# Hybrid decoder layer on one core: the recurrence's outputs computed in two token halves inside the mixing block

## The reference

```
y     = wkv7_scan(r, decay, k, v, kk, a)          # 8 heads x 64, state S: S = S*w + sa kk*a + v k, y = S r
mu    = mean(y over the 64 of a head); var = mean((y-mu)^2)
yn    = (y - mu) * rsqrt(var + GN_EPS) * lnx_g + lnx_b
bonus = sum(r * k * r_k over a head) * v
y_rwkv = (yn + bonus) * g                          # g = sigmoid(xg) @ gate_g2
mix   = concat(y_rwkv, y_mla) @ w_out              # y_mla: causal attention, 8 heads x 64
x     = LayerNorm(ALPHA * x + mix)
x     = LayerNorm(ALPHA * x + relu(x @ w_ffn1)^2 @ w_ffn2)
```

## Time and profile before

| what | value |
|---|---|
| time, median of 3 runs | 1475.28 us (1472.87 to 1477.7) |
| the profiled execution's own time | 1473.56 us |
| its span | 1471.8 us |
| PE busy | 1393.8 us, 95% |
| DVE, ACT, POOL busy | 917.3, 451.8, 463.6 us |
| mean granted TensorE clock | 0.972 |

### The profile page before, as it was taken

One profiled execution on the slowest core, in us unless ns is written; L12 is line 12 of the kernel. 1 busy time (PEld: TensorE's weight loads), 2 busy tenths in 40 slices (PEclk: granted clock), 3 DMA queues, 4 the chain that ended last, 5 costly groups with the idle time before them and its releaser, 6 DMA issues. The chain is left out here.

```text
span 1471.8 us, 24860 instructions
## 1 busy us (share of the span) xinstructions
PE 1393.8 (95%) x10608; PEld 1145.3 (78%) x10608; DVE 917.3 (62%) x1017; ACT 451.8 (31%) x619; POOL 463.6 (32%) x285
## 2 busy tenths in 40 slices
PE   6999999888999979999789988999999999999997
PEld 5877878766777669997478876888888888888886
DVE  3547745254465424434747778777777685778887
ACT  2133533122433433232300352222121353433330
POOL 0000212120133110000105658666667344455030
PEclk8999999988999989999989999999999999999999
DMA  5111234486447952221061205444443897655653
GB/s 206 43 50 38 110 133 143 139 179 212 114 115 243 232 136 46 46 47 60 0 228 43 101 29 179 157 158 157 150 158 122 291 329 267 193 187 198 201 189 126
DMA packets 144830, 211.80 MB, mean 144 GB/s; under 512 B 79472, under 2 KB 82160, under 8 KB 144080
## 3 DMA queue, kind: packets, MB, share of 16 engines
q1 hardware_dynamic: 144528, 209.69, 44.9%
q10 hardware_dynamic: 192, 0.52, 0.2%
HBM read 136.18 MB, written 64.29 MB: 136 GB/s over the span
## 5 line engine op out<-in xcount | busy, mean ns | idle before, releaser
L2342 PE MATMUL banks<-stage_b_hi,stage_a_hi 128*128 128x512 f32 x448 | 174.3, 389 | 0.0
L2342 PE MATMUL banks<-stage_b_lo,stage_a_hi 128*128 128x512 f32 x448 | 174.3, 389 | 0.0
L2342 PE MATMUL banks<-stage_b_hi,stage_a_lo 128*128 128x512 f32 x448 | 174.3, 389 | 0.0
L2584 DVE TENSOR_TENSOR stage_a_lo<-stage_a_raw,stage_a_hi 128x1024 fp32r<-128x1024 f32 x56 | 98.7, 1762 | 38.7 <-ACT stage_a_hi L2438 38.7
L358 PE MATMUL banks<-xT_hi,win_hi 128*128 128x512 f32 x320 | 103.5, 405 | 4.7 <-DVE xT_lo L705 4.7
L358 PE MATMUL banks<-xT_lo,win_hi 128*128 128x512 f32 x320 | 100.4, 395 | 0.0
L358 PE MATMUL banks<-xT_hi,win_lo 128*128 128x512 f32 x320 | 100.0, 394 | 0.0
L2342 PEld LDWEIGHTS banks<-stage_b_hi,stage_a_lo 128*128 128x128 f32 x448 | 84.1, 188 | 17.6
L2342 PEld LDWEIGHTS banks<-stage_b_hi,stage_a_hi 128*128 128x128 f32 x448 | 84.1, 188 | 17.5
L2342 PEld LDWEIGHTS banks<-stage_b_lo,stage_a_hi 128*128 128x128 f32 x448 | 84.1, 188 | 17.3
L2438 ACT ACTIVATE stage_a_hi<-stage_a_raw 128x1024 fp32r<-128x1024 f32 x56 | 59.4, 1060 | 117.8 <-DMA stage_b_raw<-in_w_ffn 97.7
(11 more groups left out here) (404 smaller groups left out, 3683.5 us busy)
## 6 DMA issues: line engine op xcount, KB each, us to landing
stage_b_raw<-in_w_ffn SPq DMA_DIRECT2D x50, 512.0 KB, 4.7
hid_s<-tile_s SPq DMA_DIRECT2D x64, 256.0 KB, 4.3
stage_a_raw<-hid_s SPq DMA_DIRECT2D x32, 512.0 KB, 3.7
w_landed<-in_w_ffn SPq DMA_DIRECT2D x30, 512.0 KB, 5.1
hid_h<-tile_h SPq DMA_DIRECT2D x48, 256.0 KB, 2.0
stage_a_raw<-hid_h SPq DMA_DIRECT2D x24, 512.0 KB, 3.8
win_raw<-in_w_in SPq DMA_DIRECT2D x20, 512.0 KB, 3.7
x_tok<-in_x SPq DMA_DIRECT2D x8, 512.0 KB, 8.0
```

Of the source, the lines that this page charges most:

```text
L2342: last = nc.tensor.matmul(ps[:, bank, :], s[a][:, j, tok], s[b][:, j, :], start=p == 0 and j == 0 and n == 0, stop=p == NP - 1 and j == 1 ...
L2584: V.tensor_tensor(s["a_lo"][:], s["a_raw"][:], s["a_hi"][:].bitcast(F32), ALU.subtract).then_inc(lo2, 1)
```

## The change

1. `rwkv_chunks`: `v` is turned to tokens by `centre`, the identity less 1/64 within a head, so the values are centred on entry; TensorE waits once for VectorE to make it. The outputs go into an own tile `y_all`. SP loads three row tiles of `w_out` at the end of its list.
2. The block `rwkv_outputs` is gone. Its work stands in `mix_ffn`, in two halves `h` of 512 tokens, without the means and their subtraction. The dot product is written over `hT`'s key rows and the bonus over its value rows.
3. The row tiles of `w_out` are taken in the order 4, 5, 6, 7, 0, 1, 2, 3, attention's first. Their high parts are made by ScalarE, their low parts by VectorE; three raw tiles are held.
4. Token tiles 0 and 1 are mixed while the first half's outputs are made; the second half's outputs stand between the products of tiles 2 and 3. Tiles 2 to 7 take the banks that come free.
5. The low parts of the outputs are all made by VectorE; GpSimd has none of them.
6. SP loads `x` in two halves, the first one ahead of the row tiles 3 to 7 of the new order, and the rows of the LayerNorm and the first feed-forward weights after the last output.

```diff
-                        last = mm(ps[own[p], B_V, cols(c)], hT[own[p], T_V + c, now(m)], k.eye[own[p], :],
+                        last = mm(ps[own[p], B_V, cols(c)], hT[own[p], T_V + c, now(m)], centre[own[p], :],
...
+            V.tensor_scalar(centre[:], k.eye[:], -1.0 / HD, None, ALU.add).then_inc(centred, 1)
...
-            for kt in range(AHEAD, KT):
-                sp.wait_ge(w_split, kt - AHEAD + 1)
-                sp.dma_start(w_raw[kt % AHEAD][:], t["w_out"][kt]).then_inc(w_in[kt % AHEAD], 16)
+            sp.wait_ge(dot_in, RT)
+            sp.dma_start(x1[:, 0:4, :], xt[:, 0:4, :]).then_inc(x_in, 16)
+            for i in range(AHEAD, KT):
+                sp.wait_ge(w_split, i - AHEAD + 1)
+                sp.dma_start(w_raw[i % AHEAD][:], t["w_out"][W_ORDER[i]]).then_inc(w_in[i % AHEAD], 16)
+            sp.wait_ge(dot_mm, 2 * RT)
+            sp.wait_ge(x_in, 16)
+            sp.dma_start(x1[:, 4:TT, :], xt[:, 4:TT, :]).then_inc(x_in, 16)
+            sp.wait_ge(gn_done, 2 * RT)
...
+            def early(i):
+                pe.wait_ge(w_split, i + 1)
+                for tt in range(2):
+                    products(tt, (W_ORDER[i],))
...
-            for kt in range(KT):
-                pe.wait_ge(w_split, kt + 1)
-                for tt in range(4):
-                    last = products(tt, 2 * tt, (kt,))
+            dots(0)
+            early(0)
+            dots(1)
+            variance(0, 0)
+            variance(0, 1)
...
+            for c in range(RT):
+                if c < 2:
+                    gate(0, c + 2)
+                    spreading(0, c + 2)
+                else:
+                    dots(RT + c - 2)
+                pe.wait_ge(yr_lo_done, c + 1)
+                pe.wait_ge(w_split, 5 + c)
+                for tt in range(2):
+                    last = products(tt, (c,))
...
+            pe.wait_ge(mixed, 1)
+            products(2, W_ORDER[:4])
+            for c in range(2):
+                gate(1, c)
+                spreading(1, c)
+            products(2, W_ORDER[4:]).then_inc(mix_mm, 1)
...
+            def out_low(i):
+                dve.wait_ge(w_whi, i + 1)
+                V.tensor_tensor(w_lo[:, W_ORDER[i], :], w_raw[i % AHEAD][:], w_hi[:, W_ORDER[i], :].bitcast(F32), ALU.subtract)\
+                    .then_inc(w_split, 1)
...
+            for c in range(RT):
+                out_step(0, c)
+                if c:
+                    out_low_part(0, c - 1)
+                    out_low(3 + c)
```

More of the change, by code:

```diff
@@ L1510, in _ @@
             sp.wait_ge(gate_in, 16)
+            sp.wait_ge(state_ready, 12)
+            for j in range(3):
+                sp.dma_start(k.wout_raw[j][:], k.w_out[4 + j]).then_inc(w_out_in, 16)
+            sp.wait_ge(w_out_in, 48)
         @block.tensor
@@ L1955, in mix_ffn @@
     w_lo = mem.at("wout_lo", 158, [P, KT, D], F32R)
-    w_raw, AHEAD = k.wout_raw, len(k.wout_raw)
+    w_raw, AHEAD = k.wout_raw[:3], 3
+    hT, cols, y_all, ones_block = k.hT, k.cols, k.outputs_from, k.ones_block
+    square = [mem.at(f"dev_square{j}", 86 + 2 * j, [P, HALF]) for j in range(2)]
+    full = [mem.at(f"yr_full{j}", 203 + 2 * j, [P, HALF]) for j in range(2)]
+    scale = mem.at("gn_scale", 4.625, [P, RT, TT, 2])
+    gn_eps = mem.at("gn_eps", 4.5, [P, 1])
+    W_ORDER = (4, 5, 6, 7, 0, 1, 2, 3)
+    DOT_BANK, GATE_BANK, VAR_BANK = (4, 5), (6, 7), 6
+    var_of = ps[:, VAR_BANK, 0:RT * TT * 2].rearrange("p (c t h) -> p c t h", c=RT, t=TT)
     x_hi, x_lo = k.x1T_hi, k.x1T_lo
@@ new lines, in out_done @@
+            def out_done(h, c):
+                n = RT * h + c
+                act.wait_ge(gn_done, n + 1)
+                A(k.yr_hi[:, c, half[h]], full[n % 2][:], COPY).then_inc(yr_hi_done, 1)
+            act.wait_ge(e_init, 1)
+            squares(0, 0)
+            squares(0, 1)
+            out_high(0)
+            squares(0, 2)
+            squares(0, 3)
+            out_high(1)
+            out_high(2)
+            gn_roots(0)
+            widen(0, 0)
+            widen(0, 1)
+            out_high(3)
@@ new lines, in _ @@
+            for c in range(RT):
+                out_done(0, c)
+                if c < 2:
+                    widen(0, c + 2)
+                out_high(4 + c)
+            for c in range(RT):
+                squares(1, c)
+            gn_roots(1)
+            widen(1, 0)
+            widen(1, 1)
+            for c in range(RT):
+                out_done(1, c)
+                if c < 2:
+                    widen(1, c + 2)
+            act.wait_ge(init, 1)
+            root(0)
+            root(1)
@@ new lines, in out_low_part @@
+            def out_low_part(h, c):
+                n = RT * h + c
+                dve.wait_ge(yr_hi_done, n + 1)
+                V.tensor_tensor(k.yr_lo[:, c, half[h]], full[n % 2][:], k.yr_hi[:, c, half[h]].bitcast(F32), ALU.subtract)\
+                    .then_inc(yr_lo_done, 1)
+            dot_step(0)
+            out_low(0)
+            for c in range(1, RT):
+                dot_step(c)
+            bonus_step(0)
+            bonus_step(1)
+            out_low(1)
+            bonus_step(2)
```

314 lines of the change are left out of this document (167 added, 147 removed).

## The result

| | before | changed |
|---|---|---|
| median of the comparison runs | 1476.49 us (1472.87 to 1478.3, 4 runs) | 1457.57 us (1455.06 to 1463.41, 4 runs) |
| profiled execution's own time | 1473.56 | 1463.41 |
| start of the outputs | 686.5 | 691.6 |
| outputs to the turns of the first half (the stretch) | 131.3 | 116.0 |
| from the turns to the end | 653.9 | 653.9 |

The ratio is 0.9881 with a 95% interval of 0.9843 to 0.9918: some 17.5 us faster (12 to 23), where 17.4 was forecast. Of the 13.7 us at half rate before, TensorE waited through 7. The profiled execution of the changed kernel was the slowest of its four, so the same kernel was profiled again (first experiment); the stretch agrees there within 0.4 us.

A forecast was written before the change was run, and what follows sets the result against it. TensorE, busy 95% of the span, was taken as the bound. The walk's 20.2 us, less 1.3 for switches and 1.5 for the clock, gave 17.4: 1475.28 - 17.4 = 1457.9 us, 8-in-10 range 1452 to 1467 us.

The forecast's parts named there:

- The wait of 12.3 us: TensorE's largest wait around the outputs before the change, ended by the first low part of `w_out`; forecast to go.
- what is saved before it is saved at the end: Behind token tile 6 both kernels run the same lists, so the stretch's saving reaches the end if other engines keep up.
- the second half only moves the wait: Case: each half's outputs have the whole's latency, so the wait moves behind tile 1; within 4.4 us of before, chance 0.04.
- the switches: TensorE's changes between float32 and fp32r in the stretch: 13 places at 0.1 us, 1.3 us taken off the gain.
- the walk: Engine lists followed from 686.5 us: first half 43.0 us work, 6.3 waits; tile 6 ends at 797.7, 20.2 us earlier.
- The forecast of the second half: From 735.8 us on TensorE has no wait, with 61.8 us of work until tile 6 ends.
- between none and three falls I take one, 1.5 us: TensorE's clock falling to half rate in the changed stretch: 0 to 5 us possible, 1.5 us taken off the gain.
- the fourth case: Clock case: TensorE at 0.50 from 686.5 to 735.8 us, 17.8 us slower than before, 1493 us; chance 0.05.
- centring costs nothing in the recurrence: Turning `v` with another constant keeps the same products in the recurrence, with one wait for that constant; no cost.
- is there, loaded during the recurrence: Attention's first raw row tile of `w_out` is already loaded when ScalarE makes its high part by 688.8 us; no load cost.
- four turns of the scale: TensorE's pace for the outputs' scale turns: 1.0 us for four, 8.0 us for eight turns of the scale.
- the late rows of `w_out`: Case: `x` ahead of the fourth row tile delays ScalarE and the first half's outputs; gain 4.5 to 12 us, chance 0.12.

The follow-up runs named there:

- first experiment: The changed kernel run and profiled again with no edit: median 1458.13 us, ratio 0.9881 to the kernel before.
- filled kernel: The changed kernel with 20 products that nobody reads added where TensorE waits: median 1458.02 us, ratio 0.9886 to the kernel before.
- dense and filled kernels: Changed kernel with start reordered so TensorE waits less (1456.28 us), with 20 unread products added (1458.02), or reordered with 12 unread products (1455.59).
- the loads are spread as well: Changed kernel with the start reordered and the recurrence's three `w_out` loads issued one per chunk: 1458.74 us, ratio 0.9891 to the kernel before.

## Why the prediction was right, and which sizes were off

**The mechanism.** The wait of 12.3 us is gone, token tile 6 ends 116 us behind the start and not 131, and the tail is the same, 653.9 us, as the step "what is saved before it is saved at the end" had it. That the second half only moves the wait is refuted by the unbroken 61.63 us behind 746.05. The 15.3 us of the stretch can be put together as an estimate: 6.8 of work for the means, 9.8 of waits (15.2 less 5.4), less 1.8 because more of the time at half rate fell on work (it cost up to 3.3 us before and 5.1 after); 0.5 stays over. No single part carries it. By the runs, the centring is the largest (15.5 us in time when it alone is undone), the order of the row tiles next (2 to 7 us), and the low parts on VectorE give 3.5 us in the old structure but no more than about 2 in the new one (0.9896 against 0.9881, 0.3 us in the stretch). These can't be added up: GpSimd's slowing of VectorE counted before because TensorE waited for VectorE's whole list, and most of that wait is gone by other means.

**TensorE's work and waits.** 49.3 us were forecast for the first half and 54.42 came (746.05 - 691.63). Of the 5.1 us too many, 5.2 are the three groups at half rate; the rest of the sum stood, with work of 43.8 us (the switches in it) for 43.0 and waits of 5.4 for 6.3. From the start on these were 1.3, 1.0, 2.0, 0.2, 0.2 and 0.6 us, where the walk had 1.4, 1.3, 2.3, 0.4, 0.3 and 0.6. (The 336 products of the list of work are 7 x 10.88 = 76.2 us and not 76.4; the walk, which the forecast uses, is not touched by it.) The forecast of the second half was 0.2 off.

**The clock, mis-sized.** The step was "between none and three falls I take one, 1.5 us". Three came, for 5.2 us. The step took the variances in shorter groups as seen without a fall at 694 in the earlier trace rows, but up to 706 TensorE waited at most 0.3 us there. In the changed kernel the first two falls, 4.0 and 14.2 us after the start, came right behind waits of 1 to 2 us; the third, at 21.1 us, came behind eight variance products and a wait of 0.24 us only. The filled kernel had the same work with little waiting and no fall at all. So with the idle time the falls went too; how much of it a fall takes isn't shown, and the falls of one list differ from execution to execution (6.8 to 13.7 us at half rate in the profiles where the start of the block wasn't edited). The Trainium skill, "TensorE: Matmul & The Clock Gate", section "HAM oscillation — how this bites in real kernels", has short bursts of products between longer waits for transfers as the cause of repeated falls. The trace agrees with that only in part: here falls came with waits of 2.1 us and less, and 0.83 as mean clock over the first 30 us is not the half rate throughout that the fourth case took.

**The early loads, costed at nothing.** This step failed. The words were that centring costs nothing in the recurrence and that the raw tile "is there, loaded during the recurrence", without a price for loading it there. Added alone to the kernel before, these loads cost 3.4 us (1.6 to 5.2); in the changed kernel the fourteenth chunk was 0.8 and 4.5 us longer in the two profiles, and not at all where they were taken away. The times of the packets on q8 point at late instructions, as said above. Taking the loads away is no cure, though: loaded at the start of the block, the row tiles made the kernel 7.8 us slower. The centring itself shows no cost there: the other chunks are 9.4 to 10.0 us in both kernels.

**The switches and the turns.** 13 x 0.1 us were taken off. The fourth group shows the 0.1 (2.84 against 2.73), but four turns of the scale took 718.79 - 717.89 = 0.90 and 720.46 - 719.65 = 0.81 and not 1.0: their pace was the one that the prediction took from a duration (2.05) and not from the distance of two starts. With eight of these, 0.8 to 1.5 us come back. In the stretch, 15.3 us were gained in the first profile (14.9 in the second) and not 17.4: the clock term was 3.7 too small (5.2 against 1.5), the waits 0.9 too large, and work with the switches some 0.6 too large. The median came out as forecast all the same, so the sum is better than its terms, and that is luck.

**The other engines.** `x`'s first half landed in 7.6 us where I took 11, no row tile of `w_out` took over 8.5, and the late rows of `w_out` did not come. GpSimd began 86.2 us behind the start, not 82.5 (777.8 and 769 by the clock of each), and TensorE never waited for it. So nothing of theirs reached the path, as forecast.

**What stays open.** From profile to profile the gain is 15.3 us, from median to median some 17.5: the medians of before are above its profiled execution by 1 to 3 us, and there is only its one trace. And the stretch 5 to 7 us shorter in the dense and filled kernels shows in the medians with 2.5 us at most, and with none where the loads are spread as well: in their profiles the block starts at 689.2 to 689.5, 3.4 to 3.7 us later than in the changed kernel's second one. 0.7 to 2.3 us of that lie ahead of the recurrence's first chunk and the rest in its chunks, none of them edited but by the spread loads.

## What to carry to other kernels

Where an early list alternates short products with waits of 1 to 2 us, price the half rate of each such place from the trace, and either pack it (work that waits for nothing goes first) or keep TensorE busy in the waits; each made the stretch 5 us of 116 shorter here, of which the medians show too little to tell it from nothing. A linear correction such as a mean belongs at the entry of a recurrence, in a constant that is multiplied anyway: it takes away not just its own work but the hand-over that everything behind it waits for. Here that was worth about twice its work. And a load placed "in the shadow" of a dense stream of tiny products is not free until a run with that load alone says so; look at the packets of the instruction queue beside it.

## What the hardware showed unexpectedly

- Three loads of 512 KB inside the recurrence: in eight of eleven profiles with them TensorE paused for 0.55 to 2.7 us, always 2.3 to 2.5 us behind the start of an instruction packet that came 5.1 to 7.5 us after the one before. Alone they made the kernel before 3.4 us slower (1.6 to 5.2).
- Twenty more products made the stretch 5.1 us shorter, because the granted clock stayed at 1.00.
- One list ran with 6.8, 10.2 and 13.7 us at half rate in three executions.
- VectorE's step of two tiles in memory, 128x1024, takes 1.28 us alone and 3.37 beside GpSimd; of 128x512, 0.75 alone and up to 1.83 beside it.
